# First mixers of a two-block transformer: weight products as three single passes over split fp32 words, in chunks through four buffers

## What is computed

```
proj = h @ w_in                       # 256x1024 @ 1024x2304: q 512, k and v 256, gate_b, gate_c, u 512 each
q, k, v, gate_b, gate_c, u = split(proj)
y_attn = windowed attention(rope(q), rope(k), v)          # 8 heads of 64, 2 kv heads
y_conv = gate_b * centred_short_conv(gate_c * u, conv_w)  # width 512
y = concat(rmsnorm(y_attn, g_attn), rmsnorm(y_conv, g_conv))
x = x + y @ w_out                     # 256x1024 @ 1024x1024
x = x + hierarchical_moe(rmsnorm(x))  # 32 experts, 2 for a token, all 32 read
```

## Time and profile before

| | |
|---|---|
| three runs | 1985.08, 1985.64 (median), 1987.7 us |
| profiled execution | 1982.81 us; its span from first to last instruction 1981.0 us |
| mean granted TensorE clock | 0.988 |
| PE busy | 1890.3 us (95%), 10968 products' records |
| DVE, ACT, POOL busy | 755.9, 614.6, 267.6 us |
| first mixer and router, layer 0 | from the start to 148.25 us |
| experts, layer 0 | 148.25 to 602.3 us |
| first mixer and router, layer 1 | 602.3 to 744.9 us |
| experts, layer 1 | 744.9 to 1199.0 us |
| second block | from 1199.0 us |

### The profile page before, as it was taken

The page is one execution under the profiler, slowest core; times in us unless marked ns, Lnnn a source line. Parts: engine busy times, 40 slices in busy tenths (PEclk is TensorE's granted clock), DMA queues, the critical chain, the costliest instruction groups (busy, mean ns, idle before and its releaser), DMA issues.

```text
span 1981.0 us, 27126 instructions
## 1 busy us (share of the span) xinstructions
PE 1890.3 (95%) x10968; PEld 1245.4 (63%) x10968; DVE 755.9 (38%) x1751; ACT 614.6 (31%) x1178; POOL 267.6 (14%) x247
## 2 busy tenths in 40 slices
PE   8999999999998999999999999999999989999997
PEld 6764444444446754444444446888889968788996
DVE  3333122211212333122111214556665644756665
ACT  2312111111112312111111113456555444574653
POOL 1400000000000400000000003871000057600000
PEclk9999999999999999999999999999999999999999
DMA  9458999999998357999999995452435744433353
GB/s 364 155 195 336 416 427 427 428 428 429 428 413 296 132 206 327 419 427 427 428 429 429 428 424 199 156 205 76 153 101 170 263 141 168 168 128 104 114 177 117
DMA packets 121423, 557.50 MB, mean 281 GB/s; under 512 B 5008, under 2 KB 49584, under 8 KB 96240
## 3 DMA queue, kind: packets, MB, share of 16 engines
q1 hardware_dynamic: 119696, 551.51, 70.4%
q10 hardware_dynamic: 1440, 4.36, 0.6%
q0 software_dynamic: 192, 0.30, 0.1%
HBM read 555.11 MB, written 1.05 MB: 281 GB/s over the span
## 4 chain that ended last, share of the span: by engine, by line
PE 84%; DMA 6%; ACT 4%; DVE 4%; issue 2%; POOL 0%; SPq 0%; POOLq 0%; DVEq 0%
PE bank L2071 14%; PE bank L2102 10%; PE bank L1822 7%; DMA ring<-w_up_dram 6%; PE bank L2073 6%; PE bank L1831 4%; PE bank L2216 3%; PE bank L2218 3%; PE bank L2217 3%; PE bank L2195 3%; PE bank L2196 3%; PE bank L2197 3%; PE bank L1814 3%; PE bank L1910 3%; PE bank L2274 3%; PE bank L2045 3%
## 5 line engine op out<-in xcount | busy, mean ns | idle before, releaser
L2071 PE MATMUL bank<-ring,work 128*64 128x512 f32 x544 | 242.5, 601 | 10.6 <-issue 10.6
L2073 PE MATMUL bank<-ring,work 128*64 128x512 f32 x512 | 230.6, 605 | 0.0
L758 POOL TENSOR_TENSOR w_lo<-ring,w_hi 128x512 fp32r<-128x512 f32 (+1 forms) x160 | 208.6, 1324 | 78.7 <-ACT w_hi L954 76.4
L1472 DVE TENSOR_TENSOR work<-work,bank 64x512 f32<-64x512 f32 x64 | 43.9, 686 | 446.0 <-ACT work L909 446.0
L714 POOL TENSOR_TENSOR stat<-stat,power 128x1 f32<-128x1 f32 (+1 forms) x18 | 10.8, 602 | 1493.0 <-DVE stat L1116 1457.9
L909 ACT ACTIVATE work<-bank 64x512 f32<-64x512 f32 x64 | 37.9, 592 | 472.4 <-PE bank L2073 472.4
L954 ACT CAST w_hi<-ring 128x512 fp32r<-128x512 f32 (+1 forms) x208 | 123.3, 606 | 130.8 <-PE bank L2218 86.9
L2102 PE MATMUL bank<-ring,work 128*64 128x512 f32 x480 | 155.8, 595 | 1.8 <-ACT work L914 0.4
L2071 PEld LDWEIGHTS bank<-ring,work 128*64 128x64 f32 x544 | 73.1, 138 | 122.3 <-issue 120.4
L1691 DVE TENSOR_TENSOR w_lo<-ring,w_hi 128x512 fp32r<-128x512 f32 (+1 forms) x176 | 116.1, 678 | 79.3 <-ACT w_hi L1067 79.1
L1822 PE MATMUL bank<-hT,ring 128*128 128x256 f32 x640 | 143.6, 379 | 0.0
(11 more groups left out here) (326 smaller groups left out, 4089.0 us busy)
## 6 DMA issues: line engine op xcount, KB each, us to landing
ring<-w_in_dram SPq DMA_DIRECT2D x34, 2048.0 KB, 8.4
ring<-w_gate_dram SPq DMA_DIRECT2D x34, 2048.0 KB, 20.6
ring<-w_up_dram SPq DMA_DIRECT2D x32, 2048.0 KB, 26.1
ring<-w_down_dram SPq DMA_DIRECT2D x30, 2048.0 KB, 25.6
ring_tail<-w_down_dram SPq DMA_DIRECT2D x18, 2048.0 KB, 23.6
work<-w_gate_dram SPq DMA_DIRECT2D x16, 2048.0 KB, 19.1
work<-w_up_dram SPq DMA_DIRECT2D x16, 2048.0 KB, 25.9
ring_tail<-w_up_dram SPq DMA_DIRECT2D x16, 2048.0 KB, 27.1
```

What stands on the lines that cost most here:

```text
L758: pool.tensor_tensor(w_lo[:, g % CHUNKS, 0:n], w[:, k], w_hi[:, g % CHUNKS, 0:n], ALU.subtract).then_inc(chunk_lo, 1)
L2071: pe.matmul(m_bank(m)[gate, :], lhs, wg[:, k], start=(k == 0), stop=(k == KD - 1), skip_group_check=True)
L2073: mu = pe.matmul(m_bank(m)[up, :], lhs, wu[:, k], start=(k == 0), stop=(k == KD - 1), skip_group_check=True)
```

## The change

All weight products of the first block's two mixers (the projections and the output product, layers 0 and 1) are made as the second block makes its own. ACT rounds each chunk of weights to `w_hi` (new line 864), DVE subtracts to `w_lo` (new line 1300), PE makes three products for one (new lines 1992 to 1994 and 2041 to 2043). `MIX_CHUNKS` cuts a mixer's weights into 52 chunks: 8 for q, 4 for k and v, 2 for each of 12 gate tiles, 16 for the output; all go through the four chunk buffers, and one is written again once PE has used it (`mix_left`). The activations are split too: hT by ACT (new L869) and DVE (new L1310), Y1 and the convolved rows by ACT and DVE (new L1383, L1390). A Y1 bank is now handed back by DVE and not by ACT, hT's as well. The output tiles stand in another order, with both token halves of a chunk behind each other. The chunk buffers lie in `ring_tail`, so a mixer has four places for its seven pieces. `normalise` of token half 0 before the router comes after the last output tile instead of after tile 5, the tables of the second block are made in the first turn of the experts instead of in mixer 0, and the products of zeros are 11 instead of 16 at the start and none instead of 4 before the second logits.

The diff, cut to its core:

```diff
-IDLE_START, IDLE_EXPERTS, IDLE_MIXER, IDLE_BETWEEN, IDLE_ROUTER, IDLE_PICKS = 16, 16, 4, 36, 22, 4
+IDLE_START, IDLE_EXPERTS, IDLE_BETWEEN, IDLE_ROUTER, IDLE_PICKS = 11, 16, 36, 22, 4
...
-OUT1 = [(0, 0, 1), (0, 1, 1), (0, 0, 0), (0, 1, 0), (1, 0, 1), (1, 0, 0), (1, 1, 1), (1, 1, 0)]
+OUT1 = [(hf, t, part) for hf in range(2) for part in (1, 0) for t in range(NT)]
...
-            return (4, 0, 1, 2, 3, 5, 4)[j]
+            return j % RING2
...
+        SLOT_LEFT = {0: ("gb", 3), 1: ("out1", 3), 2: ("out1", 7), 3: ("u", 3), 4: ("out1", 7), 5: ("gb", 3)}
...
-                for n in (0, 1, 2, MOE_RING, 3, MOE_RING - 1, 5, 4, 6, *range(MOE_RING + 1, TURN)):
+                for n in (3, MOE_RING, 0, 5, MOE_RING - 1, 1, 2, 4, 6, *range(MOE_RING + 1, TURN)):
...
+                def round_chunks(cs):
+
+                    for c in cs:
+                        src = mix_weights(act, layer, c)
+                        if layer * NMC + c >= CHUNKS:
+                            mix_left(act, layer, c)
+                        act.copy(mix_part(w_hi, layer, c), src).then_inc(mix_hi, 1)
...
                 if layer > 0:
+                    round_chunks(range(CHUNKS))
                     for t in range(NT):
                         act.wait_ge(moe[layer - 1]["x_ready"], t + 1)
                         square(2 * layer, t)
-                        copy_hT(2 * layer, *((0, 1) if t == 0 else (2,)))
+                        round_hT(2 * t)
+                        round_hT(2 * t + 1)
                 else:
                     for t in range(NT):
                         act.wait_ge(x_loaded[t], 16)
                         square(0, t)
-                    copy_hT(0, 0, 1, 2)
+                    round_chunks(range(CHUNKS))
+                    for j in range(4):
+                        round_hT(j)
...
             def first_mixer(layer):
                 stage = 2 * layer
-                last_hT(stage)
                 if layer == 0:
-                    second_block_tables()
+                    rest_of_chunks(layer, range(CHUNKS))
+                for j in range(4):
...
+                    dve.wait_ge(x_hi1, 4 * layer + j + 1)
+                    dve.tensor_tensor(hT_lo[:, part[0], part[1]], bank(name)[:].rearrange("p (a b) -> p a b", b=P),
+                                      hT_hi[:, part[0], part[1]], ALU.subtract).then_inc(psum_read[TILE[name] % BANKS], 1)
+                rest_of_chunks(layer, range(CHUNKS, MC_GATES))
...
                 for hh in range(HEADS):
                     if hh + 1 < HEADS:
                         logits(hh + 1)
                         weights(hh + 1)
+                    if hh == 6:
+                        for f in range(4):
+                            rest_of_conv(f)
+                    if hh % 2 == 0 and hh > 0:
+                        rest_of_y(hh // 2 - 1)
...
-                    if i == 5:
-                        S.settle()
-                        normalise(stage + 1, 0)
+                    if i in (3, 5):
+                        rest_of_chunks(layer, out_chunks((i + 1) // 2))
+                S.settle()
+                normalise(stage + 1, 0)
...
                 for t in range(NT):
-                    normalise(2 * layer + 2, t, h if layer + 1 < DEPTH else x)
+                    stage = 2 * layer + 2
+                    if layer + 1 < DEPTH:
+                        mean_square(stage, t)
+                        rest_of_chunks(layer + 1, range(t, t + 1))
+                        root_known(stage, t)
+                        scale_rows(stage, t)
...
+                if layer + 1 < DEPTH:
+                    rest_of_chunks(layer + 1, range(NT, CHUNKS))
...
+                def split_chunk(dst, x_hi, x_lo, c, kk, first, last):
+
+                    hi, lo = mix_part(w_hi, layer, c)[:, kk], mix_part(w_lo, layer, c)[:, kk]
+                    pe.matmul(dst, x_hi, hi, start=first, stop=False)
+                    pe.matmul(dst, x_lo, hi, start=False, stop=False)
+                    return pe.matmul(dst, x_hi, lo, start=False, stop=last)
...
+                for t in range(NT):
+                    turn_h(2 * layer, t, (IDLE_START if layer == 0 else IDLE_EXPERTS) if t == 0 else 0)
+                    claim(("q", layer, t))
+                    query_half(0, t)
+                for t in range(NT):
+                    query_half(1, t)
...
                     for nm, j in BESIDE_HEAD[hh]:
                         if nm == "out1":
-                            pe.wait_ge(conv_sq, 4 * layer + 4)
+                            pe.wait_ge(conv_lo, 4 * layer + 4)
```

More of the change, by code:

```diff
@@ new lines, in program, with gate_chunks, out_chunks, mix_marked @@
+        NMC = len(MIX_CHUNKS)
+        MC_KV, MC_GATES = KD, KD + 4
+        MC_OUT = MC_GATES + 2 * len(GATE_TILES)
+        def gate_chunks(i):
+            return range(MC_GATES + 2 * i, MC_GATES + 2 * i + 2)
+        def out_chunks(g):
+            return range(MC_OUT + 4 * g, MC_OUT + 4 * g + 4)
+        def mix_marked(n):
+            return sum(z[5] is None for z in MIX_CHUNKS[:n])
+        def mix_weights(eng, layer, c):
+            j, k0, nk, c0, n, _ = MIX_CHUNKS[c]
+            if j == 0 and k0 < KD // 2:
+                eng.wait_ge(q_first_half, 16 * (layer + 1))
+            else:
+                eng.wait_ge(w_loaded[f"mix{layer}"][mixer_piece(j)], mixer_count(j))
+            return piece(mixer_piece(j), KD, MIX_PIECES[j][2])[:, k0:k0 + nk, c0:c0 + n]
@@ L601, in mixer @@
                     slot = mixer_piece(j)
-                    if j == RING:
-                        full(sp, ("q", layer, 1))
+                    if j >= RING2:
+                        nm, last = (("q", 1), ("kv", 1), ("gc", 3))[j - RING2]
+                        full(sp, (nm, layer, last))
                     elif layer > 0:
@@ L898, in turn @@
                         act.copy(gathered(0), m_bank(m)[:]).then_inc(M[f"read{4 + m % 4}"], 1)
+                        if first and layer == 0 and p == 1:
+                            second_block_tables()
                         if first and p == 0:
@@ new lines, in chunk_made, with query_half @@
+                def chunk_made(c):
+                    pe.wait_ge(mix_lo, layer * NMC + c + 1)
+                def query_half(half, t):
+                    for k in range(half * KD // 2, (half + 1) * KD // 2):
+                        chunk_made(k)
+                        ts = slice(t * P, (t + 1) * P)
+                        mm = split_chunk(bank(("q", layer, t))[:], hT_hi[:, k, ts], hT_lo[:, k, ts], k, 0, k == 0, k == KD - 1)
+                        if k == KD - 1:
+                            done(mm, ("q", layer, t))
+                        elif t == NT - 1:
+                            mm.then_inc(mix_used, 1)
@@ new lines, in _ @@
+                for t in range(NT):
[4 more added lines that the diff above has]
+                    query_half(1, t)
+                for t in range(NT):
+                    claim(("kv", layer, t))
+                for c in range(4):
+                    chunk_made(MC_KV + c)
+                    for t in range(NT):
+                        ts = slice(t * P, (t + 1) * P)
+                        for kk in range(2):
+                            k = 2 * c + kk
+                            mm = split_chunk(bank(("kv", layer, t))[:, 0:2 * KVW], hT_hi[:, k, ts], hT_lo[:, k, ts],
+                                             MC_KV + c, kk, k == 0, k == KD - 1)
+                        if c == 3:
+                            done(mm, ("kv", layer, t))
+                    if c < 3:
+                        mm.then_inc(mix_used, 1)
@@ L1871, in gate_tile @@
                 def gate_tile(nm, j):
-                    w_ = arrive({"gc": 2, "u": 3, "gb": 4}[nm])
                     name = (nm, layer, j)
                     claim(name)
-                    done(by_feature(bank(name)[:, 0:SEQ], w_, j), name)
+                    dst = bank(name)[:, 0:SEQ]
+                    for half, c in enumerate(gate_chunks(GATE_TILES.index((nm, j)))):
+                        chunk_made(c)
+                        for kk in range(KD // 2):
+                            k = half * KD // 2 + kk
+                            hi, lo = mix_part(w_hi, layer, c)[:, kk], mix_part(w_lo, layer, c)[:, kk]
+                            pe.matmul(dst, hi, hT_hi[:, k], start=(k == 0), stop=False)
+                            pe.matmul(dst, hi, hT_lo[:, k], start=False, stop=False)
+                            mm = pe.matmul(dst, lo, hT_hi[:, k], start=False, stop=(k == KD - 1))
+                        if half == 0:
+                            mm.then_inc(mix_used, 1)
@@ L1877, in _ @@
+                    done(mm, name)
                 gate_tile("gc", 0)
```

161 lines of the change are left out of this document (106 added, 55 removed).

## The result

Four runs of the changed kernel took 2008.86 to 2011.59 us, median **2010.38 us**; four of the kernel before beside them 1986.47 us. The ratio is 1.0122, with a 95% interval of 1.0107 to 1.0137: the change makes the kernel slower by 23.9 us. The forecast was slower by 14.3 us (1999.9, range 1984 to 2011). The profiled execution took 2010.16 us, with a span of 2008.2 us and a mean granted clock of 0.973 (0.988 before).

What follows compares the result with a forecast made beforehand. The prediction took PE's products to bound the mixers. Waits less savings, +5.9 us, and the clock, +8.4, made +14.3: 1982.8 became 1997.1 profiled, plus 2.8 for the median, 1999.9 us, range 1984 to 2011.

Steps and rivals of the forecast that it cites:

- the clock: Half clock behind four waits of 6 to 7 us, two at starts, two before the output: 2.1 us each, +8.4 us.
- Rival (a): New products run as densely as fp32 passes, 0.218 and 0.108 us: 10.7 us less, 1989.2 us; chance 0.10.
- Start of layer 0: q starts at 16.9 us against 14.22, its second half waits 0.9 + 1.7; less the savings, +1.05 us.
- Start of layer 1: Before q, +6.2 us from rests and normalisation, +0.9 for the second half's transposes, less 4.45 saved: +2.65 us.
- Heads: Mixer heads: copies of q and k stand behind casts on ACT, +0.9 us; Y1's banks handed back later, +3.2 us.
- Y1's banks: In the heads, DVE hands each bank back up to 3.3 us later, paid twice; taken as 1.6 us each.
- Rival (c): Clock holds; waits at Y1's banks and the output's chunk rests are covered by DVE: -6.7 us, 1978.9; chance 0.11.
- First output tile: PE stands 7.2 us before it, for ACT's squares and DVE's rests of the convolved rows; +5.8 us taken.
- Output tiles 4 and 6: Each waits for a rest that begins after the addition of tile 3 or 5: 1.55 us each, +3.1 us.
- The waits' sum: Both mixers at full clock, waits less savings: 1.05 + 2.65 + 2.2 = +5.9 us.
- Rival (e): Clock falls fully at four long waits, 13.6, and about four short ones, 6.8: +26.3 us, 2011.9; chance 0.12.
- What costs nothing: Fewer mixer slots, moved second-block tables, fewer starting zeros and weight issues on SP add no time; experts' stage stays as long.

Runs made afterwards that it cites:

- e1_zeros: The changed kernel with 26 products of zeros in each of TensorE's four long waits, before q and before the first output tile; 2003.52 us, ratio 1.0085.
- e11_zeros_moved: The kernel of e9_all_zeros with its seven products of zeros before the first scores put ahead of the waits for q's and k's copies; 2002.86 us, ratio 1.008.
- e10_scores_zeros: The kernel of e2_order with zeros in its remaining waits, those before the first scores ahead of the waits for q's and k's copies; 1964.25 us, ratio 0.989.
- e3_before_wait: The kernel before the change with the last hT tile's copy made eleven times in both mixers, so TensorE stands before q's second half; 2005.12 us, ratio 1.0101.
- e9_all_zeros: The changed kernel, in its own order, with products of zeros in nearly all TensorE waits except those for Y1's banks; 2009.53 us, ratio 1.0118.
- e2_order: The changed kernel with the same work in another order on ACT and DVE, transposes ahead of q, no zeros added; 1974.13 us, ratio 0.9936.

## Why the forecast was right and where it was wrong

The sign, the place and the mechanism were right. The size was too small above all by two terms: the clock, 8.4 us where some 14.6 were lost, and the waits in the heads, about 2 us a layer.

**The products.** 0.227 and 0.120 us, as worked out from the earlier trace rows. Rival (a), dense products, is out, and so are the 216 and 109 ns of the Trainium skill (TensorE: Matmul & The Clock Gate, section "Wait — 56ns, not 53.3ns?") for this form of product.

**Start of layer 0.** Forecast 16.9, measured 17.13; second half 1.7, measured 1.6.

**Start of layer 1.** From the zeros behind the experts to q it was 6.75 us; forecast 6.2 more, measured 13.5, so 6.8 more. The forecast took the chunk's rest ahead of each normalisation as hidden by the inverse root. It was not: the first normalisation began 3.93 us after those zeros' start instead of 3.54, the second 9.33 instead of 8.54, 0.4 us for each rest.

**Heads.** Scores +0.9, measured 1.9 against 1.0. Y1's banks, two times 1.6: measured 2.2 and 1.7. Rival (c), that DVE comes in time, is out.

**First output tile.** Forecast 7.2, measured 6.6. Sum of squares +0.5, measured 1.6 against 1.0. Output tiles 4 and 6: forecast 1.55 each, measured 1.53. Router +0.2, measured 0.6.

**The waits' sum.** Forecast +5.9 us. What the clock cost in the change can be read from stretches that another kernel ran at the full clock. In layer 0, from q's first product to the first scores it took 31.17 us against 28.62 in e1_zeros (2.5 us); from there to the first Y1 bank as long as without (0); from the second Y1 bank (90.34) to the first output tile 19.38 against 17.89 in e11_zeros_moved (1.5); from there to the sum of squares 12.31 against 10.01 in e1_zeros (2.3); over the router's zeros 1.0. That is 7.3 us, and the stretches of layer 1 are alike to 0.1 us: as an estimate 14.6 for both. Of the 27.4 us by which the profiled mixers grew 12.8 are left for the waits less the savings, 5.5 in mixer 0 (forecast 2.15) and 7.3 in mixer 1 (3.75). Most of this excess is in the heads. From the first scores to the first output tile the kernel before took 54.67 us. At the full clock the change would take 26.8 + 15.2 + 17.9 = 59.9, so 5.2 more, where the forecast's terms (3.2 + 5.8, less 5.75 saved in ten gate tiles) give 3.3. The forecast priced single waits there, and the stretch went at DVE's pace.

**The clock.** This is the term that was sized worst: "The change makes four waits of 6 to 7 us [...] I take 2.1 each: +8.4". The long waits themselves were nearly right: 5.1 to 5.6 us of products at half clock behind each, worth 2.5 and 2.3 us by the stretches above, 9.7 together. But six shorter stretches were priced at nothing: four in the heads behind waits of 1.9 and 2.2 us, worth 0 and 1.5 in each layer, and two in the routers, 1.0 each, 5.0 us together. Rival (e) had short stretches too, and its 2011.9 is 1.5 us from the median. It was given 0.12. Its sum came out partly by luck: 13.6 for the long stretches and 6.8 for the short ones are both too much, and the heads' waits were too small in it as in the forecast. The trace of the kernel before held the warning. The prediction read the fall behind 403.2 as one behind less than 2 us of standing; PE in order of time has 2.17 us, the size of the waits in the heads:

```profile
404.95 0.77 PE L2071 MATMUL bank<-work 128*64 128x512 f32 x1 [2.17 <-DMA ring<-w_up_dram]
...
463.72 0.61 PE L2071 MATMUL bank<-ring,work 128*64 128x512 f32 x1 [2.21 <-issue]
```

Layer 0's experts have four such waits of 2.2 us. Half clock follows three of them (from 405.25, 494.00 and 552.00, 3.5 us each) and not the one that ends at 463.72.

**What costs nothing.** Layer 0's experts 449.9 against 450.1 us and the whole second part unchanged: the fewer slots for the weights and the moved tables cost nothing outside the mixers.

**Where the expected gain went.** The passes save 33.9 us, and e10_scores_zeros shows that the change can keep most of it: 21 us. The change as it was made lost it by the places of its rests: the rests of h behind both halves' normalisation and all first chunks, those of the convolved rows behind head 7's softmax, and four chunk rests behind an addition.

## What to carry to other kernels

Splitting products moves work from TensorE to engines that run in a fixed order, and each new rest is paid by the place it gets in that order, not by its duration; an engine's idle time between two steps of a softmax is such a place. Price a new wait of TensorE with the products that come behind it, short waits of 2 us too, if the trace has a row where the clock fell after one. Then ask what ends the stretch that the half clock falls in: where another engine does, it costs less than half, or nothing. Zeros that are to bridge a wait must stand ahead of the instruction that waits, in a bank that is already free, and count a little under the wait.

## What the runs showed of the hardware

- TensorE stood from about 13.4 us in e3_before_wait; the granted clock was still 1.00 until 16.25, fell to 0.50, and was back 5 us after the products began. In the changed kernel an open wait of 1.9 us before the first scores was followed by 3.5 us at 0.52 (50.00 to 53.50).
- The same wait brings a fall in one program and not in another. The 1.9 us wait at a Y1 bank had one behind it in e9_all_zeros (94.50) and none in layer 0 of e11_zeros_moved, where PE ran the same products.
- Falls can come elsewhere once some waits are filled: e1_zeros had none behind its long waits and 7 us instead of 3.5 in each router. They differ between executions of one kernel as well: its four had mean clocks of 0.981 to 0.984 and took 2000.85 to 2006.93 us.
- In layer 0's experts of the kernel before, three waits of 2.2 us had 3.5 us of half clock behind them and a fourth had none.
- What a stretch of half clock cost depended on what ended it: 2.5 us for the 5.6 us of products at q's start (31.17 against 28.62), 1.0 us for 3.5 us of zeros in the router (6.62 against 5.62), and nothing in the first heads (26.84 against 26.81), where DVE set the pace.
- From e2_order to e10_scores_zeros 30.1 us of half clock went, 9.3 of them zeros. The mixers became 6.9 and 5.1 us shorter and layer 0's experts 1.5 us longer (450.0 and 451.5), which no run explains; the medians are 9.9 us apart.
